# Attention scores of two heads in two row halves of the array, keys and queries reloaded in place

## What is computed

```python
# layer 0, group B: z = q k^T * scale, for queries t of a block and keys < t
log_keep = where(causal, log_sigmoid(-z), 0)
suffix = cumsum(log_keep, from the last key) - log_keep
a = where(causal, exp(log_sigmoid(z) + suffix), 0);  out = a @ v
# layer 1, group C: 256 keys chosen for each query by the indexer
s = q_lat . c_sel * scale - slope[h] * dist;  p = softmax(s);  o_lat = p @ c_sel
```

## Time and profile before

| what | us |
|---|---|
| median of three runs | 3840.8 |
| the profiled execution | 3842.63 |
| its span, first to last instruction | 3840.7 |
| TensorE busy | 3558.8 (93%) |
| VectorE busy | 2259.5 (59%) |
| ScalarE busy | 1961.1 (51%) |
| POOL busy | 763.4 (20%) |

### The profile page before, as it was taken

How to read it: one execution, slowest core, us unless ns; L and a number is a source line. 1 busy time by engine, 2 the same in 40 slices (tenths; PEclk the granted TensorE clock), 3 DMA queues, 4 the chain that set the end, 5 groups by cost and what they waited for, 6 DMA issues and landing times. The chain is left out here.

```text
span 3840.7 us, 83061 instructions
## 1 busy us (share of the span) xinstructions
PE 3558.8 (93%) x32524; PEld 3088.6 (80%) x32524; DVE 2259.5 (59%) x5752; ACT 1961.1 (51%) x4396; POOL 763.4 (20%) x785
## 2 busy tenths in 40 slices
PE   5999999989899989979779999986899999999899
PEld 5777899978788878867557987976788888888787
DVE  6100100057788873320799999968777777777422
ACT  5222211146666652212677667554677777777411
POOL 3222100012566640002005425315100000000000
PEclk9999999989999999989899999988999999999999
DMA  5332311198433423452313354346644443342432
GB/s 191 111 123 106 132 64 64 46 189 197 100 74 79 105 79 127 147 202 93 89 41 130 113 168 143 101 161 210 148 101 101 90 101 87 85 97 60 139 123 81
DMA packets 336556, 441.63 MB, mean 115 GB/s; under 512 B 18344, under 2 KB 255528, under 8 KB 326824
## 3 DMA queue, kind: packets, MB, share of 16 engines
q1 hardware_dynamic: 271416, 343.72, 33.7%
q10 hardware_dynamic: 64768, 92.81, 6.5%
HBM read 272.37 MB, written 164.10 MB: 114 GB/s over the span
## 5 line engine op out<-in xcount | busy, mean ns | idle before, releaser
L1331 PEld LDWEIGHTS s_o<-s_v,s_pT 128*64 128x64 f32 x13056 | 402.0, 138 | 86.0 <-issue 62.0
L1331 PE MATMUL s_o<-s_v,s_pT 128*64 128x64 f32 x13056 | 436.7, 224 | 16.6 <-issue 16.6
L215 PE MATMUL s_acc<-s_wh,s_hT 128*128 128x256 f32 (+1 forms) x1408 | 429.5, 305 | 6.3 <-ACT s_parts L638 3.1
L216 PE MATMUL s_acc<-s_wl,s_hT 128*128 128x256 f32 (+1 forms) x1408 | 428.1, 304 | 0.0
L217 PE MATMUL s_acc<-s_wh,s_hT 128*128 128x256 f32 (+1 forms) x1408 | 428.1, 304 | 0.0
L1498 ACT ACTIVATE s_probs<-s_probs,s_nmx 128x512 f32<-128x512 f32 (+3 forms) x640 | 417.2, 658 | 11.2 <-DVE s_nmx L1544 11.2
L1316 PE MATMUL s_s<-s_kh,s_qs 128*128 128x512 f32 (+3 forms) x944 | 377.1, 403 | 39.2 <-DMA s_qs<-fm 16.8
L215 PE MATMUL s_acc<-s_hT,s_wh 128*128 128x512 f32 x880 | 350.9, 399 | 56.4 <-DVE s_wl L314 26.0
L1533 DVE CUSTOM_DVE_ANT_0 s_probs<-s_s,s_scores 128x512 f32<-128x512 f32 (+3 forms) x640 | 371.6, 607 | 8.3 <-PEq L91 7.1
L2301 DVE TENSOR_SCALAR_CACHE_REDUCE s_scratch<-s_scores,s_thr 128x384 uint8<-128x384 f32 (+4 forms) x320 | 365.3, 1210 | 1.1
L216 PE MATMUL s_acc<-s_hT,s_wh 128*128 128x512 f32 x880 | 347.7, 395 | 0.0
(11 more groups left out here) (253 smaller groups left out, 7536.3 us busy)
## 6 DMA issues: line engine op xcount, KB each, us to landing
fm<-s_parts ACTq DMA_DIRECT2D x120, 512.0 KB, 2.8
s_qs<-fm SPq DMA_DIRECT2D x58, 512.0 KB, 6.5
s_y<-y SPq DMA_DIRECT2D x32, 640.0 KB, 5.9
y<-s_g SPq DMA_DIRECT2D x18, 1024.0 KB, 5.6
kc<-s_parts SPq DMA_DIRECT2D x32, 512.0 KB, 3.3
s_kh<-kc SPq DMA_DIRECT2D x30, 512.0 KB, 10.7
s_kl<-kc SPq DMA_DIRECT2D x30, 512.0 KB, 12.2
s_w<-in_o_fm SPq DMA_DIRECT2D x25, 512.0 KB, 4.6
```

Of the source, the lines that this page charges most:

```text
L215: nc.tensor.matmul(out, sh, mh, start=(j == 0), stop=False)
L216: nc.tensor.matmul(out, sh, ml, start=False, stop=False)
L1331: last = nc.tensor.matmul(o_ps[r:r + HD, 0:HD], pT[:, x * P + r:x * P + r + HD], v[:, g.u.kbs[g.a + x], vc:vc + HD], start=(g.first and x ...
```

## The change

- Queries and keys stand as they are in memory: a tile `qh`, `ql`, `kh` and `kl` each with the first head of the pair in rows 0 to 63 and the second in rows 64 to 127. The scores of two heads for the same block are six matmuls over 64 rows, high x high, low x high, high x low, each for the first head and then the second, into two PSUM banks. One semaphore step of two is given at the end of all six.
- The units of the two heads are listed together and their groups alternate; blocks go 0, 1, 2, 3, 15, 14 down to 4, and in both stages a unit's latest group comes first.
- There is one set of the four tiles. It is loaded in parts of 512 columns: a part is reloaded for the next pair once the last block that reads it is scored, part 3, then 2, then 1; part 0 alternates with a spare tile of 512 columns.
- In a batch the four scores (two pairs) stand in a row after the first two transposed groups. ScalarE's and VectorE's orders are as before. In the sparse stage `LEAD` and `R` become 16 (12 before), `US` 32 (16).
- The causal mask is four matmuls of 64 columns over 64 rows for the two heads, from `not_after` and `masked`, which POOL and VectorE make at the start; VectorE waits for POOL there.
- The value matmul's start flag is given by the first head alone.

```diff
+BLOCKS = [0, 1, 2, 3, *range(NT - 1, 3, -1)]
+def paired_groups(pairs):
+    units, out = [], []
+    for j in range(pairs):
+        for b in BLOCKS:
+            both = [Unit(j, hh, b, list(range(b + 1))) for hh in range(2)]
+            parts = chunks(b + 1, GB)[::-1]
+            for u in both:
+                u.ng = len(parts)
+            for n, (a, m) in enumerate(parts):
+                for u in both:
+                    g = Group(len(units) + u.hh, u, a, m, n == 0, n == len(parts) - 1)
+                    g.part, u.end = n, len(out)
+                    out.append(g)
+            units += both
+    return units, out
...
+    def load_part(self, sp, p, part):
+        arrived = self.part_in[4 if part == 0 and p % 2 else part]
+        for n, d in enumerate(self.rows):
+            sp.dma_start(self.tile(n, p, part).bitcast(F32),
+                         d[p * P:(p + 1) * P, part * BANK:(part + 1) * BANK]).then_inc(arrived, 16)
...
+    def score(self, nc, gs, banks, stop=True):
+        for n, (q, k) in enumerate(((0, 2), (1, 2), (0, 3))):
+            for g, bank in zip(gs, banks):
+                u, half = g.u, slice(g.u.hh * HD, (g.u.hh + 1) * HD)
+                query = self.tile(q, u.j, u.b // GB)[half, u.b % GB * P:(u.b % GB + 1) * P]
+                last = nc.tensor.matmul(bank[:, 0:g.m * P], query, self.tile(k, u.j, g.a // GB)[half, 0:g.m * P],
+                                        start=(n == 0), stop=(n == 2 and stop))
+        return last
...
-                                    start=(g.first and x == 0), stop=(g.last and x == g.m - 1),
+                                    start=(g.first and x == 0 and g.u.hh == 0), stop=(g.last and x == g.m - 1),
...
-    NG, LEAD, EXP_LEAD, R, US, BATCH, TB = len(gs), 12, 6, 12, 16, 4, 8
+    NG, LEAD, EXP_LEAD, R, US, BATCH, TB = len(gs), 16, 6, 16, 32, 4, 8
...
+                        ahead.load_part(sp, p + 1, 0)
+                        load_values(p + 1)
+                        for part in (3, 2, 1):
+                            sp.wait_ge(scored, p * PER_PAIR + freed_at[part])
+                            ahead.load_part(sp, p + 1, part)
...
                     if k >= 4:
-                        pe.wait_ge(biased, k - 3)
+                        pe.wait_ge(biased, k - 2)
...
                 for n in range(0, NG, BATCH):
-                    for a in range(n, n + BATCH, 2):
-                        turn(a)
-                        turn(a + 1)
-                        if a + LEAD < NG:
-                            score(a + LEAD)
-                            score(a + LEAD + 1)
+                    turn(n)
+                    turn(n + 1)
+                    if n + LEAD < NG:
+                        score(n + LEAD)
+                        score(n + LEAD + 2)
+                    turn(n + 2)
+                    turn(n + 3)
...
+                    if first:
+                        for x, bank in enumerate(banks):
+                            half = slice(HD * x, HD * x + HD)
+                            for part in range(2):
+                                k0 = w - P + part * HD
+                                ins = nc.tensor.matmul(bank[:, k0:k0 + HD], c.not_after[part][half, :],
+                                                       c.masked[half, :], start=False, stop=(part == 1))
+                    ins.then_inc(scored, 2)
...
                     if not g.first:
-                        dve.wait_ge(scanned, k)
+                        dve.wait_ge(scanned, k - 1)
...
+                dve.wait_ge(ordered, 1)
+                first, second = c.not_after
+                for n in range(2):
+                    v.tensor_copy(second[n * HD:(n + 1) * HD, :], first[HD:P, :]).then_inc(ordered, 1)
+                dve.wait_ge(ordered, 3)
+                v.tensor_copy(first[HD:P, :], first[0:HD, :])
```

More of the change, by code:

```diff
@@ L147, in make_constants @@
     c.identb = sc.sb("identb", [P, P], BF16)
-    c.causal = sc.sb("causal", [P, P], BF16)
+    c.not_after = [sc.sb(f"not_after{n}", [P, P], BF16) for n in range(2)]
+    c.masked = sc.sb("masked", [P, HD], BF16)
     c.window = sc.sb("window", [P, 2 * P])
@@ L1291, in __init__ @@
+class PairTiles:
     def __init__(self, nc, sc, q_rows, k_rows, vals, gates, side=None):
[L1292 to L1295, removed]
+        self.rows, self.vals, self.gates = (*q_rows, *k_rows), vals, gates
+        self.cols = [sc.sb(n, [P, S], F32R, side) for n in ("qh", "ql", "kh", "kl")]
         self.v = sc.sb("v", [P, NT, 2 * HD], F32, side)
@@ L1343, in sparse_attention @@
     slope = slopes(C_HEADS)
-    units = [Unit(h // 2, h % 2, b, list(range(b + 1))) for h in range(C_HEADS) for b in range(NT)]
-    gs = groups_of(units)
-    NG, LEAD, EXP_LEAD, R, US, BATCH, TB = len(gs), 12, 6, 12, 16, 4, 8
-    PER_HEAD, PAIRS = NG // C_HEADS, C_HEADS // 2
-    assert NG % BATCH == 0 and PER_HEAD % BATCH == 0
+    PAIRS = C_HEADS // 2
+    units, gs = paired_groups(PAIRS)
+    NG, LEAD, EXP_LEAD, R, US, BATCH, TB = len(gs), 16, 6, 16, 32, 4, 8
+    PER_PAIR = NG // PAIRS
+    assert PER_PAIR % BATCH == 0
     who, nth, _ = shares(NG, lambda k: k % BATCH == 1)
-    ends = [(u.first + u.ng - 1) // BATCH for u in units]
+    ends = [u.end // BATCH for u in units]
+    freed_at = {part: 1 + max(u.end for u in units[:2 * NT] if u.b == part * GB) for part in (1, 2, 3)}
     slot = [sum(1 for e in ends[:ui] if e == ends[ui]) for ui in range(len(units))]
@@ L1526, in bias @@
                     u, us = g.u, g.ui % US
-                    part = k - u.first
+                    part = g.part
                     if k >= R:
@@ L1548, in output @@
                     u, us = units[ui], ui % US
-                    last = u.first + u.ng - 1
                     p = u.j
-                    dve.wait_ge(exp_made, last + 1)
+                    dve.wait_ge(exp_made, u.end + 1)
                     d = rsum[:, us, 0:1]
@@ L1584, in stick_breaking @@
 def stick_breaking(nc, c, fm, vals, gates, y_dram, ahead, tiles):
-    units = [Unit(h // 2, h % 2, b, list(range(b + 1))) for h in range(B_HEADS) for b in range(NT)]
-    gs = groups_of(units, latest_first=True)
+    PAIRS = B_HEADS // 2
+    units, gs = paired_groups(PAIRS)
     NG, LEAD, SCAN_LEAD, R, BATCH, TB = len(gs), 8, 6, 12, 4, 8
-    PER_HEAD, PAIRS = NG // B_HEADS, B_HEADS // 2
+    PER_PAIR = NG // PAIRS
     CAP = 4 * S
-    assert NG % BATCH == 0 and PER_HEAD % BATCH == 0
-    ends = [(u.first + u.ng - 1) // BATCH for u in units]
+    assert PER_PAIR % BATCH == 0
+    ends = [u.end // BATCH for u in units]
+    freed_at = {part: 1 + max(u.end for u in units[:2 * NT] if u.b == part * GB) for part in (1, 2, 3)}
     slot = [sum(1 for e in ends[:ui] if e == ends[ui]) for ui in range(len(units))]
@@ L2783, in trunk @@
             q0, k0 = (FM0[name] * P for name in ("qb", "kb"))
[L2784 to L2785 removed]
+            ahead = PairTiles(nc, sc, [fm0[n, q0:k0, :] for n in range(2)],
+                              [fm0[n, k0:k0 + B_HEADS * HD, :] for n in range(2)], vb, gb, side="right")
             short_attention(nc, c, [window_heads(fm0, va, ga, y0, 0), window_heads(fm0, va, ga, y0, 1),
@@ L2848, in trunk @@
             q0 = FM1["qc"] * P
-            ahead = FirstHead(nc, sc, [fm1[n, q0:q0 + HD, :] for n in range(2)], [kc[n, 0:HD, :] for n in range(2)],
+            ahead = PairTiles(nc, sc, [fm1[n, q0:q0 + C_HEADS * HD, :] for n in range(2)], [kc[n] for n in range(2)],
                               vc, gc)
```

200 lines of the change are left out of this document (85 added, 115 removed).

## The result

The changed kernel takes 3896.2 us, median of four runs (3894.3 to 3897.8), against 3841.0 (3831.6 to 3841.8) for the one before: a ratio of 1.0149, interval 1.0132 to 1.0167, so 55 us slower. The prediction was 3861: right in sign and within its range of 3768 to 3905, with an increase of 20 where 55 came, and outside the 3835 to 3885 that it gave the forecast itself.

A forecast was written before the change was run, and what follows sets the result against it. TensorE was taken to bound both stages, the stick-breaking one with VectorE little behind. Sparse +7, stick-breaking +10 and the rest +3 gave +20: 3862.6 us, 3861 as median, eight in ten within 3768 to 3905.

The forecast's parts named there:

- waits that go: TensorE, both stages: scores between transposes cover the copies, so idle time is gained, 15 us sparse and 8 stick-breaking.
- three phases for four matmuls: Scores of two heads: three phases of paired 64-row matmuls replace four matmuls, gaining 64 us sparse and 32 stick-breaking.
- changes of shape (mask included): TensorE: two more tile-shape changes a batch at 0.095 us, 30 us sparse, 15 stick-breaking; causal mask 5 more.
- waits on VectorE: TensorE waits for VectorE's outputs in the sparse stage, 56 us, and its scans in the stick-breaking stage, 30 us.
- Side by side: Scores: a phase's two row tiles run together, so six matmuls of a 512 pair start within 0.7 us.
- serial weight loads: Rival in the scores: the two row tiles' loads follow each other, 37 us more, 3898 in all; chance 0.17.
- no overlap: Rival in the scores: row tiles don't run side by side, six phases for three, about 4080 us; chance 0.05.
- The rival without waits on VectorE: Both stages: outputs and scans are ready in time, -86 us, 3775; chance 0.28.
- Output waits: Sparse stage: value matmuls idle on VectorE's outputs about 48 times, 1 us each, six a pair; 56 us.
- the example's 4.36 less 3.45: Sparse batch: VectorE's second output ends at 4.36 us, TensorE's feed is ready at 3.45; wait given as 0.95.
- Scan waits: Stick-breaking stage: a batch's second pair of scores waits for scans in nine of twenty batches; 30 us, bounds 0 and 42.
- The credit of one batch's wait against the next: Stick-breaking stage: a wait lengthens its own batch, giving the next time in hand; 10.4 us a pair counted as 7.5.

The follow-up runs named there:

- the kernel with whole rows and no waits: Against a kernel with outputs first and scans over half their columns: each score matmul over all 128 rows, four in place of six; 3811.9 us.
- the orders are mended: Changed kernel with VectorE's outputs before copy and biases (sparse), and a pair of scores after each two transposed groups (stick-breaking); 3793.8 us.
- two and two: Changed kernel with a pair of scores after each two transposed groups, in both stages; 3884.5 us.
- the stick-breaking kernel: Kernel before with only its stick-breaking stage changed, the sparse stage as it was; 3861.5 us.
- the sparse kernel: Kernel before with only its sparse stage changed, VectorE's outputs ahead of its copy and biases; 3810.4 us.
- after: The changed kernel as first measured, against the kernel before; 3896.2 us.
- the last kernel: Changed kernel with a pair of scores after each two transposed groups in both stages, and outputs first in the sparse stage; 3868.4 us.

## Why the prediction was right or wrong

Steps against what the runs show, in us against the kernel before. "Measured" comes from the stages of the kernels above: "waits that go" is the kernel with whole rows and no waits against before (809.4 against 826.0; 417.0 against 425.2, where the mask's split into two matmuls of 64 columns is in it too).

| step | sparse, forecast | measured | stick-breaking, forecast | measured |
|---|---|---|---|---|
| three phases for four matmuls | -64 | -64, from starts: phases stand 0.23 and 0.12 apart, as matmuls did | -32 | -32 |
| changes of shape (mask included) | +30 | +55 | +20 | +23 |
| waits that go | -15 | -17 | -8 | -8 |
| waits on VectorE | +56 | +70 | +30 | +47 |
| sum | +7 | +44 (stage: +43.0) | +10 | +30 (stage: +28.8) |

- **Side by side: right.** The two matmuls of a phase start within 0.03 us of each other at every width, 128 columns too. So the rivals on serial weight loads and on no overlap are out, though the total is 2 us from the first one's 3898: it got there by other costs, and that is chance. The rival without waits on VectorE is out by its 96 waits; it becomes nearly true once the orders are mended (3793.8 against its 3775).
- **Changes of shape: the step that failed first,** in its size: 0.19 us a batch was forecast for the two new ones and 0.35 came, 55 us in the sparse stage for 30. Their count was right: two more in a batch, and two and two would have been more. The price of 0.095 came from the one place of the earlier trace rows where a score's stream ends at the value matmuls, 0.33 in place of 0.23. That is the way out. The way in was called about as much on the strength of 64 value matmuls, but the way into row tiles costs 0.17, and the first transposes behind them 0.06 more. The bounds reached 0.2 a change and held it. The step as it was put for the reader, that the first score after a transpose would start 0.1 later, reads 0.17 to 0.18.
- **Output waits: right in place, cause and number** (48 of about 1 us: 48, 58.7 us recorded). The six of a pair are 1.4, 1.0, 2.0, 0.47, 1.2 and 1.1 us long, in the six batches named, where 1.3, 0.95, 1.7, 0.6, 1.1 and 1.3 stood; the example's 4.36 less 3.45 is 0.91 and not 0.95, which changes nothing. The step failed in what a recorded wait doesn't hold, the clock behind the longest and the modelled ends: 56 forecast, 70 paid.
- **Scan waits: right in kind, too small.** 35 recorded, 47 paid, 30 forecast; the bound of 42 didn't hold. The credit of one batch's wait against the next took it from 10.4 a pair to 7.5; without the credit it would have been 42, and the runs show 47, in 12 waits a pair where nine were forecast. That is 12 of the 17 us; where the other 5 come from is not shown.
- **Waits that go: the number by luck.** The step took all idle time of before, 17 and 9 us, for transposes that wait for a copy. The waits of before in the two marked stretches say otherwise (these two rows are the sparse stage's):

```profile
PE s_o L1331 <- issue: 11.2, 10, 1.9
PE s_t L1322 <- ACT s_pT L1485: 1.8, 4, 0.6
```

Transposes waiting for copies are 1.8 us here, 1.7 more on VectorE's copies and 0.7 in the stick-breaking stage. Most of the idle time, 11.2 and 5.4 us, is pauses of TensorE in the middle of value matmuls for which the profile shows no cause. They return in the kernels that keep a stage as it was (the sparse stage of the stick-breaking kernel, the stick-breaking stage of the sparse kernel) and are nearly gone where a stage is in the new form. The gains of 17 and 8 us were measured, but why the pauses went is open.
- **VectorE's share above 85% in the stick-breaking stage: wrong.** It is 352.8 of 454.0, 78%, as the stage grew and VectorE had 353 us of work and not the 367 of before.
- **"I am wrong if the sparse stage is over 850": met.** It is 869, with overlap and parallel loads, so as a sign of their absence it was wrong.
- **Part reloads: right.** No wait on a DMA stands inside the stages, with 416.6 MB moved. The start: TensorE's first matmul comes 2.0 us later (15.3 to 17.3), and with the old tables it comes at 15.1 (sparse stage alone).
- **All other stages unchanged: off by 19 us in the trace,** on the other side. The start cost 2.0, but the stretch from the short attention's first matmul to the stick-breaking scores was 7.1 us shorter (197.5 to 190.4), the output and other projections behind it 2.8, and the stage ahead of the sparse one 9.0 (910.3 to 901.3). The first shows in the kernel with the old stick-breaking stage too (191.3), so the new loads don't make it. The last is no larger than the spread of single profiles: between the two stages, the changed kernel and the seven made from it that are alike there take 1324.5 to 1336.3 us, and the kernel before took 1339.9. The cause of the 19 is open; no run was made for it.

So the trace's increase of 53 comes about like this: the forecast's 20, three sizes of one sign (changes of shape in the sparse stage 25, output waits 14, scan waits 17, together 56), and 22 off again, since everything outside the two stages came out at -19 where +3 stood. The two stages alone are 72 us longer where the sum had 17; that the total came nearer is luck.

## What to carry to other kernels

Before an order is chosen to save changes of tile shape, list for each instruction moved which buffer of another engine it waits on: here the row of four scores saved one change of 0.16 to 0.19 us a batch; in the stick-breaking stage it cost 0.6 of waiting (47 us in 80 batches), while in the sparse stage it paid (869.0 against 889.6 us), and most once VectorE did its outputs first (798.7). Each stage wanted its own order (3793.8 us with the two, against 3841 before and 3896 with the change as it was). And take the price of a change in each direction from a place that has that direction; a recorded wait is a lower bound of what it costs.

## What was not expected of the hardware

- A change from 128-row to 64-row tiles costs 0.17 us ahead of the first score, the way back 0.09 and then 0.06 in the first transposes; with the change, six phases and the eight transposes on each side take 3.63 us (1.02, 1.59, 1.02) where eight whole-row matmuls take 3.75. The Trainium skill (TensorEngine Tiling (Array Packing), Key Properties) has the drain at a change of mode; the size is these rows'.
- Two 64-row tiles load and run in parallel even at 128 columns, where single loads already stood 0.12 us apart: three phases of 128 columns stand 0.11 us apart. The same section says that different tiles load and multiply in parallel, and the trace agrees.
- Single idle times of 1.5 to 2.0 us, in a stage that is otherwise full, can be followed by a fall of the clock: in after behind five of eight (3.77 us at a granted 0.55 behind the one shown), in the last kernel behind seven. Each such fall cost 1.7 us, so these waits cost nearly twice their recorded length.
